# A gated delta rule stage: substitution moved to GpSimd, gates turned to tokens before the softplus, copies reordered

## What is computed

```
qkv = silu(causal_depthwise_conv(qkv, conv_w))        # 32 tiles of 128 features
beta = sigmoid(b)
g = -exp(a_log) * softplus(a + dt_bias)               # (tokens, 16 heads)
g = cumsum(g)                                         # within a chunk
decay = exp(where(causal, g_i - g_j, -inf))
a = where(strict, (k_beta @ k^T) * decay, 0)
t_inv = solve(eye + a, eye)                           # unit lower triangular inverse
u = t_inv @ v_beta ;  w = t_inv @ (k_beta * exp(g))
per chunk: v_new = u - w @ state ; o = q_g @ state + qk @ v_new ; state = ...
o = rms_norm(o) * norm_w * silu(z) ;  out = o @ w_out
```

## Time and profile before

| | |
|---|---|
| median of 3 runs | 2166.47 us (2163.2 to 2168.67) |
| the profiled execution | 2163.57 us, its span 2161.8 us |
| mean granted TensorE clock in it | 0.982 |
| TensorE (PE) busy | 2066.7 us, 96% |
| VectorE (DVE) busy | 1447.0 us, 67% |
| ScalarE (ACT) busy | 1111.4 us, 51% |
| GpSimd (POOL) busy | 49.6 us, 2% |
| delta stage, first gate panel to the block loop | 1605.9 to 1893.7 us |

### The profile page before, as it was taken

The page is one execution under the profiler, slowest core; times in us unless marked ns, Lnnn a source line. Parts: engine busy times, 40 slices in busy tenths (PEclk is TensorE's granted clock), DMA queues, the critical chain, the costliest instruction groups (busy, mean ns, idle before and its releaser), DMA issues.

```text
span 2161.8 us, 41596 instructions
## 1 busy us (share of the span) xinstructions
PE 2066.7 (96%) x15668; PEld 1928.9 (89%) x15668; DVE 1447.0 (67%) x2490; ACT 1111.4 (51%) x1802; POOL 49.6 (2%) x63
## 2 busy tenths in 40 slices
PE   7998999999999999999999999999997898999998
PEld 7897889989988899999999999999986898989997
DVE  4567777774677777775567765575668886467555
ACT  4564455554654555554454544454456665546443
POOL 1001000000020000000000000000000000000000
PEclk9999999999999999999999999999998998999999
DMA  8533465553423555555556455555543433335552
GB/s 252 170 118 108 148 208 191 186 171 120 137 98 117 178 192 187 191 179 193 183 159 212 153 194 194 170 187 183 185 168 108 145 112 99 118 132 175 191 184 97
DMA packets 118585, 350.93 MB, mean 162 GB/s; under 512 B 23504, under 2 KB 36120, under 8 KB 117952
## 3 DMA queue, kind: packets, MB, share of 16 engines
q1 hardware_dynamic: 115248, 336.27, 47.2%
q0 software_dynamic: 3216, 12.97, 2.2%
HBM read 341.85 MB, written 7.34 MB: 162 GB/s over the span
## 4 chain that ended last, share of the span: by engine, by line
PE 76%; DVE 12%; ACT 6%; issue 3%; DMA 3%; POOL 0%; SPq 0%; DVEq 0%; ACTq 0%; POOLq 0%
PE bank L2108 23%; PE bank L2110 22%; PE bank L2109 22%; DVE wlo L1409 4%; ACT whi L943 3%; PE bank L2567 2%; DMA raw<-panels 1%; PE bank L2276 1%; DVE arena L1448 1%; DMA relay<-arena 1%; DVE arena L1972 1%; DVE arena L1973 1%; DVE arena L1612 1%; DMA arena<-relay 0%; PE bank L2142 0%
## 5 line engine op out<-in xcount | busy, mean ns | idle before, releaser
L2108 PE MATMUL bank<-xhi,whi 128*128 128x256 f32 x3496 | 1004.4, 287 | 24.6 <-DVE arena L1612 10.1
L2109 PE MATMUL bank<-xlo,whi 128*128 128x256 f32 x3496 | 989.5, 283 | 0.0
L2110 PE MATMUL bank<-xhi,wlo 128*128 128x256 f32 x3496 | 989.0, 283 | 0.0
L1409 DVE TENSOR_TENSOR wlo<-raw,whi 128x1024 fp32r<-128x1024 f32 x623 | 742.4, 1232 | 204.9 <-ACT whi L943 203.9
L2108 PEld LDWEIGHTS bank<-xhi,whi 128*128 128x128 f32 x3496 | 666.2, 191 | 46.3 <-DVE arena L1612 12.5
L2109 PEld LDWEIGHTS bank<-xlo,whi 128*128 128x128 f32 x3496 | 666.2, 191 | 5.4
L2110 PEld LDWEIGHTS bank<-xhi,wlo 128*128 128x128 f32 x3496 | 665.7, 190 | 0.0
L943 ACT ACTIVATE whi<-raw 128x1024 fp32r<-128x1024 f32 x623 | 623.5, 1046 | 49.4 <-DVE arena L1609 19.0
L2108 PE MATMUL bank<-whi,hhi 128*128 128x512 f32 x688 | 274.4, 399 | 2.7 <-DVE hlo L1561 1.2
L2110 PE MATMUL bank<-whi,hlo 128*128 128x512 f32 x688 | 272.8, 397 | 0.0
L2109 PE MATMUL bank<-wlo,hhi 128*128 128x512 f32 x688 | 272.5, 396 | 0.0
(11 more groups left out here) (361 smaller groups left out, 1708.5 us busy)
## 6 DMA issues: line engine op xcount, KB each, us to landing
raw<-panels SPq DMA_DIRECT2D x623, 512.0 KB, 4.3
arena<-w_in POOLq DMA_DIRECT2D x2, 2048.0 KB, 10.7
arena<-relay SPq DMA_DIRECT2D x8, 512.0 KB, 4.2
arena<-gains_in POOLq DMA_DIRECT2D x6, 512.0 KB, 4.1
relay<-arena POOLq DMA_DIRECT2D x4, 512.0 KB, 7.8
relay<-arena SPq DMA_DIRECT2D x4, 512.0 KB, 5.0
bias_table<-arena POOLq DMA_DIRECT2D x1, 1536.0 KB, 35.1
x<-x_in SPq DMA_DIRECT2D x1, 1024.0 KB, 4.8
```

The source lines that it names most:

```text
L1409: dve.tensor_tensor(wlo[slot][:], raw[slot][:], whi[slot][:].bitcast(F32), ALU.subtract) \
L2108: pe.matmul(dst, w_hi, a_hi, start=start, stop=False, skip_group_check=True)
L2109: pe.matmul(dst, w_hi, a_lo, start=False, stop=False, skip_group_check=True)
L2110: return pe.matmul(dst, w_lo, a_hi, start=False, stop=stop, skip_group_check=True)
```

## The change

- Gates: TensorE first turns four sets of rows to tokens (slot 2), VectorE does sigmoid and softplus on 128 partitions by 32, and TensorE cumulates by products with a triangular mask `until` (slot 3 for the tokens, and in `delta_rows` for the rows).
- The substitution goes from VectorE to GpSimd, with a wait between any two of its 30 instructions; ScalarE's transpose of the blocks moves from step 8 to 9 (`TURNED_AT`).
- SyncE loads one panel less ahead in each slot, and transfers the inverse in step 8 and the transposes in 9.
- ScalarE's level copies, scaled values and state (`delta_result`) stand ahead of the slot's SiLU; ScalarE rounds one panel more ahead of the gates.
- Fourteen z panels in slots 32 to 45, two in the block loop.

The diff, cut (the removed body of `delta_solve` is what GpSimd now has, `dve` for `pool`; the removed `delta_gates_turned` on VectorE is three copies and two negations of 128x32):

```diff
 NB = P // BLK
 LAST = 8 * SETS
-FIRST_Z, Z = LAST + 2, 12
+FIRST_Z, Z = LAST, 14
 SLOTS_D = FIRST_Z + Z + 1
 ROWS_AT = 4
+TURNED_AT = 9
...
-            return qd[:, f - 8, :] if f < 10 else kd[0][:, f - 10, :]
+            if f < 12:
+                return qd[:, f - 8, :] if f < 10 else kd[0][:, f - 10, :]
+            return tri_t[0][:, f - 12, :, :].rearrange("p c n -> p (c n)")
...
             def delta_inverse_over(n):
-                sp.wait_ge(d["solved"], n + 1)
+                sp.wait_ge(d["solved"], 2 * (BLK - 1) * (n + 1))
...
-                last = first_panel[s] + delta_used(t) + 3 + RING
+                last = first_panel[s] + delta_used(t) + 2 + RING
...
                     if o == 4:
                         delta_blocks_over(n)
-                    if o == 7:
+                    if o == 8:
                         delta_inverse_over(n)
-                    if o == 8:
+                    if o == 9:
                         delta_turned_over(n)
...
+                steps = BLK - 1
+                for n in range(SETS):
+                    ps, np_ = lanes(n), MATS * NB
+                    if n >= 2:
...
+                    pool.wait_ge(d["blocks_in"], 16 * (n + 1))
+                    lower = blk_t[ps, :].rearrange("p (i j) -> p i j", i=BLK)
+                    for k in range(steps):
+                        ni, nj = BLK - 1 - k, k + 1
+                        left = blk_a[ps, k * BLK + k + 1:(k + 1) * BLK].rearrange("p (i o) -> p i o", o=1) \
+                            .to_broadcast([np_, ni, nj])
+                        right = blk_t[ps, k * BLK:k * BLK + nj].rearrange("p (o j) -> p o j", o=1) \
+                            .to_broadcast([np_, ni, nj])
+                        prod = blk_tmp[ps, 0:ni * nj].rearrange("p (i j) -> p i j", i=ni)
+                        pool.tensor_tensor(prod, left, right, ALU.mult).then_inc(d["solved"], 1)
+                        pool.wait_ge(d["solved"], 2 * (steps * n + k) + 1)
+                        pool.tensor_tensor(lower[:, k + 1:, 0:nj], lower[:, k + 1:, 0:nj], prod, ALU.add) \
+                            .then_inc(d["solved"], 1)
+                        pool.wait_ge(d["solved"], 2 * (steps * n + k + 1))
...
-                act.wait_ge(d["v_turned"], 2 * SETS)
+                act.wait_ge(d["k_tail"], SETS)
+                if f >= 4:
+                    act.wait_ge(d["v_turned"], 2 * SETS)
                 if f >= 10:
                     act.wait_ge(*reached("new_sum", SETS - 2, "ks"))
+                if f >= 12:
+                    act.wait_ge(*reached("new_sum", SETS - 2, "r1"))
...
+                at = col_at[("a_log", s)]
+                act.activation(a_rate, cols[:, at:at + VH], ACT.Exp).then_inc(d["gate_act"], 1)
...
             def delta_turned_blocks(n):
-                act.wait_ge(d["solved"], n + 1)
+                act.wait_ge(d["solved"], 2 * (BLK - 1) * (n + 1))
...
-                if o == 8 + late(n):
+                if o == TURNED_AT + late(n):
                     delta_turned_blocks(n)
+                if o == 21:
+                    delta_o_copied(n)
+            def delta_result(n, o):
                 if o == 14:
                     delta_t32(n)
                 if o == 15:
@@ -1354,21 +1386,21 @@
                     delta_state(n)
...
                 if o == 20:
                     delta_scaled(n, 1)
-                if o == 21:
-                    delta_o_copied(n)
             def delta(s):
-                hi_to(first_panel[s] + 3)
+                hi_to(first_panel[s] + 4)
                 delta_gates(s)
                 for t in range(SLOTS_D):
                     if t < LAST:
                         delta_tap(s, t)
                     hi_to(first_panel[s] + delta_used(t) + 2)
+                    for n in range(SETS):
+                        delta_result(n, t - 8 * n)
                     if 1 <= t <= LAST:
                         delta_silu(s, t - 1)
                     if 0 <= t - FIRST_Z < Z:
                         delta_z(s, t - FIRST_Z)
-                    if t == 3:
+                    if t == ROWS_AT:
                         delta_gates_turned(s)
                     for n in range(SETS):
                         delta_step(s, n, t - 8 * n)
...
             def delta_gates_softplus(s):
-                a, b = slice(ROW_A, ROW_A + VH), slice(0, VH)
-                dve.wait_ge(d["gate_act"], 1)
-                link(dve.tensor_scalar(gates[b, 1, :], gates[b, 1, :], 1.0, None, ALU.add))
-                dve.reciprocal(gates[b, 0, :], gates[b, 1, :]).then_inc(d["gates_ready"], 1)
+                dve.tensor_scalar(until, masks[:, 2, :], -1.0, None, ALU.is_ge).then_inc(d["gates_ready"], 1)
+                dve.wait_ge(d["gate_turned"], 1)
                 dve.wait_ge(d["gate_act"], 4)
-                e, m, ln = gates[a, 2, :], gates[a, 1, :], gates[a, 3, :]
+                m, pre, e, ln = (gates_turned[:, v, :, :] for v in range(4))
+                by = lambda v: v.rearrange("p (c h) -> p c h", c=CHUNKS)
+                link(dve.tensor_copy(gates_turned[:, 1:, :, :].rearrange("p v c h -> p (v c h)"),
+                                     bank[7][:, CHUNKS * VH:4 * CHUNKS * VH]))
+                link(dve.tensor_scalar(m, by(bank[6][:, 0:CHUNKS * VH]), 1.0, None, ALU.add))
+                link(dve.reciprocal(beta_tok[:], m))
...
-                link(dve.scalar_tensor_tensor(out=m, in0=gates[a, 0, :], scalar=0.0, in1=ln,
-                                              op0=ALU.max, op1=ALU.add))
-                link(dve.tensor_scalar(e, m, a_rate[a, :], -1.0, ALU.mult, ALU.mult))
...
-                for c in range(CHUNKS):
-                    cs = slice(c * P, (c + 1) * P)
-                    dve.tensor_tensor_scan(g_cum[a, cs], ones[a, :], gates[a, 2, cs], 0.0, ALU.mult, ALU.add) \
-                        .then_inc(d["gates_ready"], 1)
...
+                link(dve.scalar_tensor_tensor(out=m, in0=pre, scalar=0.0, in1=ln, op0=ALU.max, op1=ALU.add))
+                dve.scalar_tensor_tensor(out=a_tok, in0=m, scalar=-1.0,
+                                         in1=a_rate.rearrange("p (o h) -> p o h", o=1).to_broadcast([P, CHUNKS, VH]),
+                                         op0=ALU.mult, op1=ALU.mult).then_inc(d["gates_ready"], 1)
+            def delta_gates_summed(s):
+                dve.wait_ge(d["gate_turned"], 2)
+                sums = bank[7][:, 256:256 + CHUNKS * VH].rearrange("p (c h) -> p c h", c=CHUNKS)
+                dve.tensor_copy(g_tok[:], sums).then_inc(d["gate_tok"], 1)
+                dve.tensor_scalar(neg_g[:], sums, -1.0, None, ALU.mult).then_inc(d["gate_tok"], 1)
+            def delta_gates_negated(s):
...
-            def delta_solve(n, first_k, last_k):
-                ps, np_ = lanes(n), MATS * NB
-                if first_k == 0:
...
@@ -2068,19 +2081,15 @@
                         delta_taps(s, t - 1)
                     if 0 <= t - FIRST_Z < Z:
                         delta_z(s, t - FIRST_Z)
-                    if t == 1:
+                    if t == 2:
                         delta_gates_softplus(s)
                     if t == 3:
-                        delta_gates_turned(s)
+                        delta_gates_summed(s)
+                    if t == ROWS_AT + 2:
+                        delta_gates_negated(s)
                     for n in range(SETS):
                         delta_step(s, n, t - 8 * n)
                     lo_to(first_panel[s] + delta_used(t) + 2)
-                    for n in range(SETS):
-                        o = t - 8 * n - late(n)
-                        if o == 6:
-                            delta_solve(n, 0, 7)
-                        if o == 7:
-                            delta_solve(n, 7, BLK - 1)
                     if t == 8 * 2 + 24:
                         delta_o_inv(0)
...
             def delta_turn_gates(s):
-                pe.wait_ge(d["gates_ready"], 3)
+                pe.wait_ge(d["gate_act"], 4)
+                pe.wait_ge(d["gates_scaled"], 2)
+                pe.wait_ge(rstd_ready, s + 1)
+                for v, (row, i) in enumerate(((0, 1), (ROW_A, 0), (ROW_A, 2), (ROW_A, 3))):
+                    rows = slice(row, row + VH)
+                    for c in range(CHUNKS):
+                        o = (CHUNKS * v + c) * VH
+                        last = pe.transpose(bank[7 if v else 6][:, o:o + VH], gates[rows, i, c * P:(c + 1) * P], ident[rows, rows])
+                last.then_inc(d["gate_turned"], 1)
+            def delta_sum_gates(s):
+                pe.wait_ge(d["gates_ready"], 2)
                 for c in range(CHUNKS):
-                    cs = slice(c * P, (c + 1) * P)
                     o = 256 + VH * c
-                    pe.transpose(bank[6][:, VH * c:VH * (c + 1)], gates[0:VH, 0, cs], ident[0:VH, 0:VH])
-                    last = pe.transpose(bank[7][:, o:o + VH], g_cum[ROW_A:ROW_A + VH, cs],
-                                        ident[ROW_A:ROW_A + VH, ROW_A:ROW_A + VH])
```

(16 more changed lines are left out.)

53 lines of the change are left out of this document (16 added, 37 removed).

## The result

The change ran at 2134.03 us, median of 4 runs (2133.8 to 2135.05), beside 2164.84 us (4 runs, 2162.81 to 2168.67) for the kernel before on the same chip: ratio 0.9857, 95% interval 0.9839 to 0.9874, 30.8 us less. The profiled execution of after took 2135.05 us, span 2133.3, mean granted clock 0.985.

The account below looks back on a forecast made before the run. TensorE, busy 96% of the span, was taken to bound the kernel. Gains of 6 + 6 + 2.3 + 4.2 + 6.2 = 24.7 us from 2163.6 gave 2138.9, plus 2.9 for the median: 2141.8, low 2132, high 2155.

Parts of the forecast that it names:

- Stretch 1: First gate panel to set 0's first inverse-level product, 72.8 us before: 6 us won, 11 at most.
- bank nothing: Gates ahead of set 0's chain: A complete near 1643, not 1650.6; the 7.5 us earlier start not counted by itself.
- Not for sets 1 to 3: TensorE does not wait for these sets' substitution: chain 30 us against a little over six slots, 38 us.
- Level copies: ScalarE copying after tap and split: 6 us won between sets 0 and 1's first level products, 2.3 the next.
- The port: GpSimd and VectorE wait for each other's instructions: 14 us a set (8 to 20), VectorE 1 to 2 more.
- The price of an operation: Each small GpSimd substitution operation: 0.28 us undisturbed, 8.4 us for the 30 of a set.
- Gate panels: Two z panels fill slots that had none, between sets 2 and 3's first level products: 4.2 us won (1 to 5).
- Block loop: After the slots, where TensorE is full: two z panels fewer, 6.2 us won (4 to 6.5).
- rival 1: Shared port makes GpSimd's substitution late, about 20 us a set: 12.7 us won, 2153.8; chance 0.2.
- rival 2: Small GpSimd operations cost nearly what the large one does, 1.19 us: 48 us lost, 2215; chance 0.06.
- rival 3: Start wins all stepped, port hardly matters: 11 and 7 us in the first two stretches, 31 won, 2135; chance 0.15.
- rival 4: Delta stage no shorter, waits on ScalarE return; only the block loop's 6.2 us stays: 2160; chance 0.06.

Follow-up runs that it names:

- gates_old: The changed kernel with gates computed by rows of 256 and scans in the old slots, table width kept: 2141.17 us, ratio 0.9874.
- sp_old: The changed kernel with SyncE's panel loads and block transfers where they were (three ahead, inverse in step 7, transposes in step 8): 2140.88 us, ratio 0.9879.
- half_more: The changed kernel with each of the 15 products of GpSimd's substitution made twice, same result: 2152.12 us, ratio 0.9926.
- copies_late: The changed kernel with ScalarE's level copies, scaled values and state back behind the slot's SiLU and squares: 2135.37 us, ratio 0.9857.
- solve_dve: The changed kernel with the substitution put back on VectorE in its old places, all else as changed: 2142.52 us, ratio 0.9897.
- pool_alone: The kernel before with nothing but the substitution moved to GpSimd: 2167.12 us, ratio 1.0010.
- shared_first: The changed kernel with the first 7 of set 0's 15 substitution steps on VectorE, the rest on GpSimd: 2125.39 us, ratio 0.9808.
- b_pad: The kernel before with 15 unused columns in the per-feature table, so later tensors lie 64 bytes further on: 2158.90 us, ratio 0.9971.

## Why the prediction was right, point by point

2141.8 was forecast with a range of 2132 to 2155; it is 2134.0, and faster, as said. The sum was 24.7. The stage itself gave 21.4 (19.3 in stretches 1 to 4, 3.1 in the block loop, less 0.9 in the fifth), so the steps together were 3.3 us too high; 7.1 that no step foresaw came from other stages. Without these the time would have been about 2141, nearly the forecast; that this is so close is partly luck, since errors inside the steps cancelled, as the points below say.

- **Stretch 1**: 6 forecast, 6.0 measured, by the chain as stepped. In after's time, which starts 5.2 us sooner, A was to be complete at 1637.8 and was at 1638.2; substitution 14, measured 15.4; transfers 8.4, measured 6.9; inverse 7.4, measured 6.9; first level 1667.6, measured 1667.4. Two errors of 1.5 cancelled, which was luck. The softplus took 2.8 us from the mask to the end, not 2.2.
- **Gates "bank nothing"**: in the sum by steps they and the transfers were folded into this chain. Undone, the gates cost 3.7 by ratio and 4.8 in stretch 1 (gates_old), the transfers 4.8 by ratio (sp_old). The second was put too low: "1.5 to 2 us a set" counts the queue only, and the transfer itself also got 1.7 to 1.9 shorter for sets 0 and 1.
- **"Not for sets 1 to 3"** failed. The chain was right (29.3 for 30), the cover was not: it was priced with slots of 6.1 us, the pitch before, while the change itself shortens those of stretch 2 to 5.5. half_more showed the cover to be gone for set 1, and to be less than the 8 us added for sets 2 and 3. At 13 to 16 us a set it cost next to nothing (0.6 us at set 1), so the time wasn't hurt.
- **Level copies**: 6 in stretch 2, measured 6.9, 2.3 in stretch 3, measured 3.0. But the cause was put in the wrong part: copies_late gives back 2.2 us by trace and nothing by ratio, solve_dve 10.5 in stretches 2 to 4. It is VectorE's freed time that ended's waits; pool_alone, where it is the only thing changed, shows 8.8 us less idle time in the same stretches.
- **The port**: "1 to 2 us a set more for VectorE" and "some splits at over 1.3" did not come: no split over 1.27, taps 1.55 to 1.61 beside 1.52., a GpSimd operation of 512 elements, were too coarse a pattern for operations of 15 to 64.
- **The price of an operation**: 0.28 each undisturbed; measured 0.28 to 0.38 from start to start (0.20 to 0.31 each and some 0.08 to the next) where VectorE leaves room. On VectorE the same operations start every 0.20 to 0.26 us (shared_first), so GpSimd is about 1.4 times slower at them. By the charge for small read commands (GPSIMD Engine Reference in the Trainium skill, Performance pitfalls), if each row were one, the first operations, of 15 to 12 rows, would have taken over 1 us, as an estimate from that figure. They took 0.20 to 0.35 us, and only the one beside a split 1.34. The estimate from the section Engine selection of GPSIMD Engine Reference in the Trainium skill (about two times slower) was 14 for VectorE's 7 us a set. The trace has 12.6 to 16.2, but with the waits for the split in it, so that the agreement is in part chance. That the move is a loss where TensorE waits for it holds for stretch 1 (2.6 us, solve_dve; 3.6 us, pool_alone), not for the whole.
- **Gate panels**: 4.2 in stretch 4, measured 3.4. **Block loop**: 6.2, measured 3.1. This is the term that was mis-sized. The panel was costed at 3.1 of a TensorE that is busy 60.9 of 61.4 us; yet a head without a panel has its own pitch of 3.56 us against 6.08, so that a panel is worth 2.5, and without panels the splits of the last heads become the wait (1.5 us more).
- **Missing from the sum**: the layout, 6 us by b_pad. In the trace of after the untouched stages but the first are 10.5 us shorter and the first hybrid stage is 3.5 longer, which makes the 7.1; b_pad has the same stages shorter by the same 10.5. The wider column table is in the diff, and it was passed over as data.

Two signs that the prediction had named as wrong came, both small: eleven of 120 GpSimd operations took over 0.7 us (1.17 to 1.38), and ScalarE's transpose of the blocks waited once for GpSimd, 1.7 us.

The rivals: GpSimd waited for VectorE's splits as rival 1 has it, but took 15.4 us for set 0 and not 20 to 22, and ScalarE's transposed blocks waited 1.7 us in all, not 2 a set; rival 2's price never came near 0.79 us; rival 3's time, 2135, is what was measured, but by another way: its 7 in stretch 2 came, its 11 in stretch 1 didn't, and the 7.1 us of other stages filled the place, which is chance; rival 4 is out.

## What to carry to other kernels

Moving short dependent work to an idle, slower engine pays through what the first engine's followers no longer wait for, and only while the chain on the slower engine stays covered; reckon that cover with the slots as they will be, not as they were. A transfer can pay twice for a bulk load issued just ahead of it: in the queue and in flight (2.35 and 1.7 us for set 0). Read idle and busy time apart: waits that end may come back as a lower clock, as in pool_alone, and then the time alone hides that the edit did what it was meant to. Before a difference is explained, see whether untouched stages changed too: here a table 60 bytes wider was worth a fifth of the gain.
